# Gate and up projections as a seven-product block scheme, with the down projection as a stage of its own

## Chip, cores, metric
The kernel runs on one core of one Trainium2 chip. The metric is the device time of one execution in microseconds.

## What is computed
One decoder layer for 1024 tokens of width 1024, float32, with a feed-forward width of 2816. The change lies in the last part, the feed-forward network:

```
h = h + mixed @ w_out
u = h * rsqrt(mean(h*h) + eps) * norm2_gain
y = h + (silu(u @ w_gate) * (u @ w_up)) @ w_down
```

Before it come a first RMS norm, one input projection, a gated linear recurrence (4 heads) and a sliding-window attention (8 heads), whose outputs (`mixed`) meet in the output projection `w_out`.

## The kernel before
Activations lie transposed: features on the 128 partitions, in 8 tiles (`KT`), tokens along the free dimension, in two halves of 512. Every large product is done in three terms for precision: each operand is split into `hi` (rounded by an ACT copy to the fp32r type) and `lo` (the rest, by a DVE subtract), and `three()` (lines 759 to 763) issues hi\*hi, hi\*lo and lo\*hi into one PSUM bank of 128x512. PSUM has eight such banks.

The engines have separate programs. A list from `schedule()` sets one order of steps, and each engine walks through it and does its part of a step: `P` and `O` are input and output projection groups on PE, `LM`, `LX`, `LV`, `OC`, `OS`, `OM`, `ON`, `OX` the recurrence, `MS`/`ML` the hi and lo parts of a mixed tile, `FD`, `F` the load and the split of feed-forward weights. The output projection has 48 groups: 0 to 31 stand between the steps of the recurrence, 32 to 47 (one k-tile each, 3 matmuls) behind the last head. SP issues all DMAs in the order of the list.

From group 32 on, `N2` steps stand between the output groups: the first gate and up weights are multiplied with the k-tiles of `u` as they get ready. `u` here is h times the gain only. The norm's factor `nrs` for each token is found beside it (ACT squares, POOL sums, a matmul with ones, ACT Ln and Exp) and is multiplied onto the gate's result by DVE (line 1248) and, after Silu, by POOL once more for the up result (line 533).

The feed-forward network then is a loop of 11 passes (`ffn`), the first and last unrolled. A pass takes two of the 22 tiles of the feed-forward width: four weight tiles (gate, up, gate, up), each 8 k-tiles x 2 token halves x 3 terms = 48 matmuls; then the hidden product's hi and lo parts stay in SBUF, and the down projection adds both tiles into 16 banks' worth of output (96 matmuls), which DVE adds onto `h` (line 1270). 288 matmuls a pass. At the end eight tiles of y are stored.

Of the kernel before, what the change touches and what calls it, by code (L numbers as in the profile page):

```python
# [5 lines left out]
ALU = mybir.AluOpType  # L21
# [7 lines left out]
P = 128  # L29
D = 1024  # L30
# [27 lines left out]
def schedule():  # L58
# [79 lines left out]
    for h in range(NH):  # L138
# [58 lines left out]
def build(nc, xT, wv, wproj, wo_a, wo_b, wo_c, wg, wu, wd, gain1, gain2, lbl, ogain, qgain, kgain, sinks, yT):  # L197
    ctx = ExitStack()
    with ctx:
# [35 lines left out]
        h = at("h", 7, [P, KT, T])  # L235
# [48 lines left out]
        def on_tmp(hh):  # L284
# [4 lines left out]
        u2hi = at("u2hi", 39, [P, KT, T], F32R)  # L289
        u2lo = at("u2lo", 91, [P, KT, T], F32R)  # L290
        nsq = at("nsq", 79, [P, 2, T])
        nacc = at("nacc", 87, [P, T])
        nrs = at("nrs", 131, [P, T])
        hidhi = at("hidhi", 71, [P, 2, T], F32R)
        hidlo = at("hidlo", 79, [P, 2, T], F32R)
        gate = [at("gate01", 87, [P, 2, HALF]), at("gate23", 123, [P, 2, HALF])]
        hid = at("hid", 127, [P, 2, HALF])
        fraw = [at(f"fraw{p}", kb, [P, KT * P]) for p, kb in enumerate((187, 191, 155, 171, 179, 167))]
# [73 lines left out]
        def down_bank(first, g):  # L372

            return ((3, 4, 5, 6), (0, 1, 2, 7))[g // 4 % 2][g % 4] if first else g % 8

        def ffn_bank(first, p, half):

            return ((3, 4), (5, 6), (0, 1), (2, 7))[p][half] if first else 2 * p + half
# [4 lines left out]
        def _(sp):  # L383
# [7 lines left out]
            for step in order:  # L391
# [18 lines left out]
                if step[0] == "MS" and step[1] < 3 or step == ("W", N_PROJ + 1):  # L410

                    i = step[1] if step[1] < 3 else 3
                    sp.wait_ge(*((s_ufree, i + 1) if i < 3 else (s_pmm, 2 * N_PROJ)))
                    for k in (i,) if i < 3 else range(3, KT):
                        sp.dma_start(h[:, k, :], xv[k, :, :]).then_inc(s_x[k], 16)
                if step[0] == "FD":
                    p = step[1]

                    sp.wait_ge(*((s_on, 3), (s_kq, 8), (s_lmm, 2 * LEVELS * NH), (s_lmm, 2 * LEVELS * NH), (s_oc, 32), (s_on, 4))[p])
                    sp.dma_start(fraw[p][:, :], (wg[0], wu[0], wg[1], wu[1], wd[0], wd[1])[p]).then_inc(s_fraw[p], 16)  # L420
            with sp.Fori(0, FT // 2 - 1) as i:
                for p in range(6):
                    sp.wait_ge(s_flo, 6 * i + (p + 1))
                    w = (wg, wu, wg, wu, wd, wd)[p]
                    j = (0, 0, 1, 1, 0, 1)[p]
                    sp.dma_start(fraw[p][:, :], w[bass.ds(2 * i + (2 + j), 1), :, :].rearrange("a p n -> (a p) n"))\
                        .then_inc(s_fraw[p], 16)
# [7 lines left out]
        def _(pool):  # L435
            n0 = [0]
# [42 lines left out]
            for step in order:  # L479
# [28 lines left out]
                elif step[0] == "LV":  # L508
# [6 lines left out]
                    else:  # L515
# [4 lines left out]
                                            ALU.subtract).then_inc(s_lvs, 1)  # L520

            for m in range(1, KT):
                pool.wait_ge(s_nsq, m + 1)
                if m > 1:
                    pool.wait_ge(s_nacc, m - 1)
                nc.gpsimd.tensor_tensor(nacc[:, :], nacc[:, :], nsq[:, m % 2, :], ALU.add).then_inc(s_nacc, 1)
            pool.wait_ge(s_nrs, 1)
            with pool.Fori(0, FT // 2) as i:
                for j in range(2):
                    for half in range(2):  # L530
                        pool.wait_ge(s_silu, 4 * i + (2 * j + half + 1))
                        gv = gate[j][:, half, :]
                        nc.gpsimd.tensor_tensor(gv, gv, nrs[:, half * HALF:(half + 1) * HALF], ALU.mult)\  # L533
                            .then_inc(s_gr, 1)

        @block.scalar
        def _(act):
# [25 lines left out]
            def value_out(g):  # L563
                n, t = g // NC, g % NC
                act.wait_ge(s_vmm, g + 1)
                nc.scalar.activation(v[:, t, n * VW:(n + 1) * VW], ps[:, g % 8, 0:VW], ACT.Copy,
                                     scale=rtok[:, t:t + 1]).then_inc(s_vev, 1)

            for g in range(V_FIRST + 1):
                value_out(g)  # L570
            for step in order:
# [139 lines left out]
                elif kind == "NL":  # L711
                    m = step[1]
                    for x2, cols in first_in_halves(m):
                        act.wait_ge(s_oadd, 32 + 2 * m + x2)
                        nc.scalar.activation(u2hi[:, m, cols], h[:, m, cols], ACT.Copy, scale=g2[:, m:m + 1])\
                            .then_inc(s_u2hi, 1)
                    if m >= 3:
                        act.wait_ge(s_nacc, m - 2)
                    dst = nsq[:, m % 2, :] if m else nacc[:, :]
                    nc.scalar.activation(dst, h[:, m, :], ACT.Square).then_inc(s_nsq, 1)  # L720
                elif kind == "F":
                    p = step[1]
                    act.wait_ge(s_fraw[p], 16)

                    act.wait_ge(*((s_on, 3), (s_lmm, 2 * LEVELS * NH), (s_lmm, 2 * LEVELS * NH), (s_oc, 32), (s_on, 4), (s_omm, 48))[p])
                    nc.scalar.activation(fhi[p][:, :], fraw[p][:, :], ACT.Copy).then_inc(s_fhi, 1)

            act.wait_ge(s_nss, 2)
            nc.scalar.activation(nrs[:, 0:HALF], ps[:, 2, :], ACT.Ln, scale=1.0 / D, bias=eps).then_inc(s_nln, 1)
            nc.scalar.activation(nrs[:, HALF:T], ps[:, 7, :], ACT.Ln, scale=1.0 / D, bias=eps).then_inc(s_nln, 1)  # L730
            act.wait_ge(s_nln, 2)
            nc.scalar.activation(nrs[:, :], nrs[:, :], ACT.Exp, scale=-0.5).then_inc(s_nrs, 1)

            def ffn(i, last):

                for j in range(2):
                    for half in range(2):
                        act.wait_ge(s_gsc, 4 * i + (2 * j + half + 1))
                        nc.scalar.activation(gate[j][:, half, :], gate[j][:, half, :], ACT.Silu).then_inc(s_silu, 1)  # L739
                    for half in range(2):  # L740
                        act.wait_ge(s_hid, 4 * i + (2 * j + half + 1))
                        nc.scalar.activation(hidhi[:, j, half * HALF:(half + 1) * HALF], hid[:, half, :], ACT.Copy)\  # L742
                            .then_inc(s_hhi, 1)
                    for p in () if last else (2 * j, 2 * j + 1):
                        act.wait_ge(s_fraw[p], 16 * i + 32)
                        act.wait_ge(s_fmm, 8 * i + (2 * p + 2))
                        nc.scalar.activation(fhi[p][:, :], fraw[p][:, :], ACT.Copy).then_inc(s_fhi, 1)  # L747
                for p in () if last else (4, 5):
# [4 lines left out]
            with act.Fori(0, FT // 2 - 1) as i:  # L753
                ffn(i, False)
# [587 lines left out]
```

## Time and profile before

| | us |
|---|---|
| time, median of 3 runs | 1255.2 (1255.13 to 1256.24) |
| span of the profiled execution, first to last instruction | 1252.1 |
| PE busy | 1220.7 |
| DVE busy | 633.8 |
| ACT busy | 377.6 |
| POOL busy | 228.9 |

The profile is of one execution; its time is known only by its span, and the median of the runs is 3.1 us over that. PE is the matmul part of TensorE, DVE VectorE, ACT ScalarE, POOL GpSimd, SP the engine that issues DMAs. Busy times are sums of instructions; consecutive matmuls overlap, so a matmul's own duration (0.39 us) is longer than the distance to the next (0.23 us).

### The profile page before, as it was taken

The numbers are of one execution on the slowest core, as the hardware profiler recorded it, in microseconds if no ns is written. First come the engines' busy times: TensorE is split into PE (matmuls) and PEld (weight loads), VectorE is DVE, ScalarE is ACT, GpSimd is POOL, SyncE is SP. The second block draws the span as 40 slices with busy tenths as digits, with TensorE's granted clock in tenths as the row PEclk, the third lists the DMA queues.
The fourth block names the chain that finished last, engine by engine and source line by source line (L and its number), as shares of the span: only waits on it lengthen the run. The fifth ranks groups of instructions, "written<-read, shape, count | busy, mean of one in ns | idle before, by whom it ended". The sixth has DMA issues, their size and how long they took to land.

```text
span 1252.1 us, 14986 instructions
## 1 busy us (share of the span) xinstructions
PE 1220.7 (97%) x5840; PEld 1005.0 (80%) x5840; DVE 633.8 (51%) x832; ACT 377.6 (30%) x578; POOL 228.9 (18%) x155
## 2 busy tenths in 40 slices
PE   4999999999999999999999999999999999999998
PEld 4898766678888788778888888888888888888887
DVE  7305576577869795656343334343443425252514
ACT  6314454554545632452212121121212121121110
POOL 6301123342533330241100000000000000101010
PEclk9999999999999999999999999999999999999999
DMA  6101100000001302211101111011111211010003
GB/s 236 50 1 52 34 17 1 18 34 35 18 35 68 148 18 88 85 51 68 68 34 44 56 34 67 34 67 34 58 42 34 66 34 67 34 67 0 0 0 134
DMA packets 20056, 63.47 MB, mean 51 GB/s; under 512 B 3121, under 2 KB 5169, under 8 KB 20017
## 3 DMA queue, kind: packets, MB, share of 16 engines
q1 hardware_dynamic: 20016, 62.94, 14.3%
q8 instruction: 26, 0.43, 0.1%
q14 instruction: 14, 0.11, 0.0%
HBM read 58.74 MB, written 4.19 MB: 50 GB/s over the span
## 4 chain that ended last, share of the span: by engine, by line
PE 88%; DVE 5%; ACT 3%; issue 2%; POOL 1%; DMA 0%; SPq 0%; DVEq 0%; ACTq 0%
PE ps L761 27%; PE ps L763 26%; PE ps L762 26%; PE ps L927 4%; PE ps L888 1%; PE ps L902 1%; PE ps L903 1%; DVE ulo L1030 1%; DVE vlo L1024 1%; POOL D L519 1%; PE ps L953 1%; DVE B L1155 1%; POOL rec L507 0%; DVE M L1188 0%; DMA x<-xT 0%
## 5 line engine op out<-in xcount | busy, mean ns | idle before, releaser
L761 PE MATMUL ps<-u2hi,fhi 128*128 128x512 f32 x704 | 274.6, 390 | 0.9 <-DVE u2lo L1237 0.9
L763 PE MATMUL ps<-u2hi,flo 128*128 128x512 f32 x704 | 273.9, 389 | 0.0
L762 PE MATMUL ps<-u2lo,fhi 128*128 128x512 f32 x704 | 273.9, 389 | 0.0
L533 POOL TENSOR_TENSOR gate<-gate,nrs 128x512 f32<-128x512 f32 x44 | 56.7, 1291 | 612.3 <-ACT gate L739 612.3
L1270 DVE TENSOR_TENSOR h<-ps,h 128x512 f32<-128x512 f32 x176 | 116.9, 689 | 81.0 <-PE ps L763 81.0
L761 PEld LDWEIGHTS ps<-u2hi,fhi 128*128 128x128 f32 x704 | 132.2, 188 | 29.7 <-DVE u2lo L1237 1.4
L763 PEld LDWEIGHTS ps<-u2hi,flo 128*128 128x128 f32 x704 | 132.2, 188 | 27.5
L762 PEld LDWEIGHTS ps<-u2lo,fhi 128*128 128x128 f32 x704 | 132.2, 188 | 27.5 <-issue 0.2
L761 PE MATMUL ps<-hidhi,fhi 128*128 128x512 f32 x352 | 136.9, 389 | 0.0
L762 PE MATMUL ps<-hidlo,fhi 128*128 128x512 f32 x352 | 136.9, 389 | 0.0
L763 PE MATMUL ps<-hidhi,flo 128*128 128x512 f32 x352 | 136.9, 389 | 0.0
L1254 DVE TENSOR_TENSOR hid<-ps,gate 128x512 f32<-128x512 f32 x44 | 30.5, 692 | 196.8 <-PE ps L763 192.7
L761 PE MATMUL ps<-uhi,whi 128*128 128x512 f32 x272 | 112.3, 413 | 0.0
L763 PE MATMUL ps<-uhi,wlo 128*128 128x512 f32 x272 | 106.8, 393 | 0.0
L762 PE MATMUL ps<-ulo,whi 128*128 128x512 f32 x272 | 106.5, 392 | 0.0
L1248 DVE TENSOR_TENSOR gate<-ps,nrs 128x512 f32<-128x512 f32 x44 | 30.2, 691 | 131.1 <-PE ps L763 124.0
L742 ACT ACTIVATE hidhi<-hid 128x512 fp32r<-128x512 f32 x44 | 27.9, 633 | 199.1 <-DVE hid L1254 199.1
L1018 DVE TENSOR_TENSOR flo<-fraw,fhi 128x1024 fp32r<-128x1024 f32 x66 | 79.5, 1245 | 9.7 <-ACT fhi L747 5.1
L761 PEld LDWEIGHTS ps<-hidhi,fhi 128*128 128x128 f32 x352 | 66.1, 188 | 13.7
L763 PEld LDWEIGHTS ps<-hidhi,flo 128*128 128x128 f32 x352 | 66.1, 188 | 13.7
L762 PEld LDWEIGHTS ps<-hidlo,fhi 128*128 128x128 f32 x352 | 66.1, 188 | 13.7
L751 ACT ACTIVATE fhi<-fraw 128x1024 fp32r<-128x1024 f32 x20 | 20.1, 1052 | 184.2 <-PE ps L763 184.2
(192 smaller groups left out, 1876.8 us busy)
## 6 DMA issues: line engine op xcount, KB each, us to landing
fraw<-wu SPq DMA_DIRECT2D x22, 512.0 KB, 4.5
fraw<-wg SPq DMA_DIRECT2D x22, 512.0 KB, 3.2
fraw<-wd SPq DMA_DIRECT2D x22, 512.0 KB, 3.8
wraw<-wproj SPq DMA_DIRECT2D x17, 512.0 KB, 3.2
x<-xT SPq DMA_DIRECT2D x8, 512.0 KB, 6.9
h<-xT SPq DMA_DIRECT2D x8, 512.0 KB, 3.8
yT<-h SPq DMA_DIRECT2D x8, 512.0 KB, 2.6
vraw<-wv SPq DMA_DIRECT2D x16, 160.0 KB, 5.7
```

Of the source, the lines that this page charges most:

```text
L519: nc.gpsimd.tensor_tensor(DD[lv % 2][:, :].rearrange("p (b l) -> p b l", l=2 * L), b4, mid, ALU.subtract).then_inc(s_lvs, 1)
L533: nc.gpsimd.tensor_tensor(gv, gv, nrs[:, half * HALF:(half + 1) * HALF], ALU.mult)\
L742: nc.scalar.activation(hidhi[:, j, half * HALF:(half + 1) * HALF], hid[:, half, :], ACT.Copy)\
L751: nc.scalar.activation(fhi[p][:, :], fraw[p][:, :], ACT.Copy).then_inc(s_fhi, 1)
L761: nc.tensor.matmul(out, whi_, xhi_, start=first, stop=False)
L762: nc.tensor.matmul(out, whi_, xlo_, start=False, stop=False)
L763: return nc.tensor.matmul(out, wlo_, xhi_, start=False, stop=last)
L927: mm = nc.tensor.matmul(ps[:, 3 + c // 4, (c % 4) * P:(c % 4 + 1) * P], lhs[:, cs], rhs[:, cs], start=True, stop=True)
L1018: nc.vector.tensor_tensor(flo[p][:, :], fraw[p][:, :], fhi[p][:, :].bitcast(F32), ALU.subtract)\
L1248: nc.vector.tensor_tensor(gate[j][:, half, :], ps[:, ffn_bank(first, 2 * j, half), :], nrs[:, half * HALF:(half + 1) * HALF], ALU.mult).th ...
L1254: nc.vector.tensor_tensor(hid[:, half, :], ps[:, ffn_bank(first, 2 * j + 1, half), :], gate[j][:, half, :], ALU.mult).then_inc(s_hid, 1)
L1270: nc.vector.tensor_tensor(hv, ps[:, down_bank(first, g), :], hv, ALU.add)\
```

## The change
The 1024 features of `u` and of a weight tile are halved, and the tokens too: `u` becomes B11, B12 (features of the first half, tokens of each half) and B21, B22. A tile of gate weights gives A11, A12, one of up weights A21, A22. The four results (gate and up, for each token half) are formed from seven products of such blocks, each 4 k-tiles x 3 terms = 12 matmuls:

- the token side needs seven operands with hi and lo parts: B11, B21 as they are, B22, and four sums t1 = B12 - B11, t2 = B22 - t1, t3 = B22 - B12, t4 = B21 - t2. They are built once, after the norm, by DVE and POOL; so `u` is now normalised itself (`norm_tile`, and for B12 an ACT copy with the gain and a POOL multiply), in place over `h`, and `h` is first stored to HBM (`hD`) and read back later into `h2`;
- the weight side needs sums per tile: POOL forms four of 128x512 (`weight_sums`), ACT and DVE split them;
- a product that serves several results is made once and copied by ACT from one PSUM bank to the next (`seed_b`, `seed_c`); later products accumulate on the copy. `keep_p5` copies product 5 to SBUF, and DVE adds it to two results (`gate_2`, `up_2`).

The first two groups are interleaved while operands are being built; from the third on a group is (1,g) (4,g-1) (5,g) (6,g) (2,g) (3,g) (7,g). The hidden product goes to HBM (`hidD`), and the down projection comes after all gate/up groups, in 11 chunks of two tiles that are read back, split by ACT and DVE (`chunk_hi`, `chunk_lo`) and multiplied; DVE adds onto `h2`. All of it is unrolled. The `N2`, `NL`, `F`, `FD` steps go; `XU`/`XG` (loads), `XS` (POOL sums), `XH`/`XL`/`XA` (splits) take their place in the last head. Of the last 16 output groups the first token half comes first.

```diff
         if last:
-            steps[5] += [("FD", 1), ("FD", 0), ("MS", 6), ("ML", 6)]
+            steps[5] += [("XU", 0), ("XG", 0), ("MS", 6), ("ML", 6)]
             order += mix(take(n_p + 32 - taken[0]), steps)
-            order += [("FD", 2), ("FD", 3), ("F", 0)]
+            order += [("XS", 0)]
             steps = [[("OC", h, c)] for c in range(NC)] + ...
-            steps[2] += [("F", 1)]
-            steps[5] += [("F", 2)]
+            steps[2] += [("XH", 0)]
+            steps[3] += [("XL", 0)]
+            steps[8] += [("XA", 0), ("XG", 1), ("XU", 1)]
...
+    order += [("XS", 1), ("XH", 1)] + [("O", 32 + g, 0) for g in range(16)]
...
+        products = [(1, 0), (1, 1), (2, 0), (2, 1), (5, 0), (5, 1), (6, 0), (6, 1), (3, 0), (7, 0), (4, 0),
+                    (3, 1), (7, 1)]
+        for g in range(2, GROUPS):
+            products += [(1, g), (4, g - 1), (5, g), (6, g), (2, g), (3, g), (7, g)]
+        products += [(4, LAST)]
+            return ((3, 4, 5, 6), (0, 1, 2, 7))[g % 2]                # banks a, b, c, e
... POOL
+            def weight_sums(g):
...
+                nc.gpsimd.tensor_tensor(sw[:, 0:HALF], uw[:, 0:HALF], uw[:, HALF:D], ALU.add).then_inc(s_sum, 1)
+                nc.gpsimd.tensor_tensor(sw[:, HALF:D], sw[:, 0:HALF], gw[:, 0:HALF], ALU.subtract).then_inc(s_sum, 1)
+                nc.gpsimd.tensor_tensor(s34[:, 0:HALF], gw[:, 0:HALF], uw[:, 0:HALF], ALU.subtract).then_inc(s_sum, 1)
+                nc.gpsimd.tensor_tensor(s34[:, HALF:D], gw[:, HALF:D], sw[:, HALF:D], ALU.subtract).then_inc(s_sum, 1)
...
+            for k in range(4):
+                pool.wait_ge(s_unb, k + 1)
+                nc.gpsimd.tensor_tensor(h[:, 1, k, :], h[:, 1, k, :], nrs[:, 1, :], ALU.mult).then_inc(s_unp, 1)
... PE
+                bank = {1: a, 2: a, 3: c, 4: b, 5: e, 6: b, 7: b}[p]
+                elif p == 5:
+                    pe.wait_ge(s_12lo, g + 1)
+                elif p == 4:
+                    pe.wait_ge(s_22lo, g + 1)
+                    pe.wait_ge(s_c22, g + 1)
+            for p, g in products[4:]:
+                product_waits(p, g)
+                if (p, g) == (4, LAST):
+                    down(0, 0)
... output projection on PE
+                    if g == 43:
+                        norm_sum(0, (0, 6, 7), 5, 8)
+                    if g == 47:
+                        norm_sum(1, (0, 5, 6, 7), 9, 16)
... ACT, one group
+                s34_hi(g)
+                seed_b(g)
+                a22_hi(g)
+                keep_p5(g)
+                gate_hi(g + 1)
+                seed_c(g)
+                s12_hi(g + 1)
+                silu_1(g)
+                silu_2(g)
... DVE: the operands, then one group
+            norm_tile(0, 0)
+            for k in range(KT):
+                if k + 1 < KT:
+                    norm_tile(0, k + 1)
+                operand_lo(k // 4, k % 4, k % 4 + 1, h[:, 0, k, :], k + 1)
+                if k == 1:
+                    gate_lo(1)
+            for c in range(2): ... t1 ...
+            for k in range(2): norm_tile(1, 4 + k)
+            for c in range(2): operand_lo(4, ...)
+            for k in range(2, 4): norm_tile(1, 4 + k)
+            for c in range(2): ... t2 ...
+            s12_lo(1)
+            for c in range(2): operand_lo(5, ...)      # then 2, 6, 3 in the same way
...
+                s34_lo(g)
+                hid_1(g - 1)
+                a22_lo(g)
+                gate_lo(g + 1)
+                s12_lo(g + 1)
+                gate_2(g)
+                up_2(g)
```

## Rows read from the trace of the kernel before

**Rows 1.** The page: busy time, share of the span and instructions of each engine.
```profile
PE 1220.7 (97%) x5840; PEld 1005.0 (80%) x5840; DVE 633.8 (51%) x832; ACT 377.6 (30%) x578; POOL 228.9 (18%) x155
```
**Rows 2.** The page: the chain that ended last, by engine.
```profile
PE 88%; DVE 5%; ACT 3%; issue 2%; POOL 1%; DMA 0%; SPq 0%; DVEq 0%; ACTq 0%
```
**Rows 3.** PE's waits, 515 to 1249: total, times, longest.
```profile
PE ps L761 <- DVE u2lo L1237: 0.9, 2, 0.6
PE ps L761 <- DVE mlo L1232: 0.7, 1, 0.7
```
**Rows 4.** Timeline of PE: start, duration, operation, idle before.
```profile
515.64 0.47 PE L761 MATMUL ps<-mhi,whi 128*128 128x512 f32 x1 [0.69 <-DVE mlo L1232]
...
1248.00 0.39 PE L763 MATMUL ps<-hidhi,flo 128*128 128x512 f32 x1
```
**Rows 5.** Timeline of DVE: the last add group of two successive passes.
```profile
1181.19 2.65 DVE L1270 TENSOR_TENSOR h<-ps,h 128x512 f32<-128x512 f32 x4 [2.71 <-PE ps L763]
...
1246.38 2.73 DVE L1270 TENSOR_TENSOR h<-ps,h 128x512 f32<-128x512 f32 x4 [2.71 <-PE ps L763]
```
**Rows 6.** One pass: busy PE, PEld, DVE, ACT, POOL, clock, DMA share, GB/s.
```profile
1056.10:1121.30 65.20, 65.20 (x290) 53.99 (x289) 25.69 (x34) 12.15 (x15) 5.16 (x4) 1.00 0.14 48
```
**Rows 7.** Groups of ACT by shape: busy, mean ns, idle before.
```profile
L747 ACT ACTIVATE fhi<-fraw 128x1024 fp32r<-128x1024 f32 x40 | 39.8, 1043 | 0.0
L739 ACT ACTIVATE gate<-gate 128x512 f32<-128x512 f32 x44 | 27.7, 632 | 158.3 <-DVE gate L1248 158.3
L684 ACT ACTIVATE rec<-ps 128x512 f32<-128x512 f32 x8 | 4.7, 591 | 17.6 <-PE ps L947 17.6
```
**Rows 8.** Groups of DVE by shape.
```profile
L1048 DVE TENSOR_TENSOR wlo<-wraw,whi 128x1024 fp32r<-128x1024 f32 x22 | 28.2, 1285 | 10.8 <-ACT whi L579 10.8
L1248 DVE TENSOR_TENSOR gate<-ps,nrs 128x512 f32<-128x512 f32 x44 | 30.2, 691 | 131.1 <-PE ps L763 124.0 <-ACT nrs L732 7.1
```
**Rows 9.** Group of POOL by shape.
```profile
L533 POOL TENSOR_TENSOR gate<-gate,nrs 128x512 f32<-128x512 f32 x44 | 56.7, 1291 | 612.3 <-ACT gate L739 612.3
```
**Rows 10.** DMA issues: KB each, median us to landing.
```profile
fraw<-wu SPq DMA_DIRECT2D x22, 512.0 KB, 4.5
```
**Rows 11.** Timelines of POOL, then DVE, where both work.
```profile
440.09 1.89 POOL L519 TENSOR_TENSOR D<-B 128x1024 f32<-128x1024 f32 x1 [2.29 <-DVE rec L1179]
455.20 2.89 POOL L519 TENSOR_TENSOR D<-B 128x1024 f32<-128x1024 f32 x1 [1.23 <-DVE M L1188]
522.95 2.55 POOL L526 TENSOR_TENSOR nacc<-nacc,nsq 128x1024 f32<-128x1024 f32 x1 [64.86 <-ACT nsq L720]
...
440.53 2.00 DVE L1188 TENSOR_TENSOR M<-K,D 128x512 f32<-128x512 f32 x1
442.45 0.68 DVE L1188 TENSOR_TENSOR M<-Q,D 128x512 f32<-128x512 f32 x1
523.16 1.28 DVE L1089 TENSOR_TENSOR h<-ps,h 128x512 f32<-128x512 f32 x2
```
**Rows 12.** Group of DVE in 10 to 34 us.
```profile
L1030 DVE SCALAR_TENSOR_TENSOR ulo<-x,small,uhi 128x1024 fp32r<-128x1024 f32 x6 | 14.1, 2356 | 0.6 <-ACT uhi L545 0.6
```
**Rows 13.** The chain in order of time: start, duration.
```profile
555.74 1.72 PE ps L989 x4
```
**Rows 14.** Two stretches; columns as in rows 6.
```profile
20.00:24.00 4.00, 1.32 (x7) 1.35 (x8) 4.00 (x2) 4.00 (x6) 3.86 (x2) 0.93 0.54 200
24.00:28.00 4.00, 2.35 (x9) 1.95 (x8) 4.00 (x2) 0.39 (x1) 3.71 (x3) 0.64 0.14 41
```
**Rows 15.** The last head: timelines of DVE and PE.
```profile
487.92 0.69 DVE L1089 TENSOR_TENSOR h<-ps,h 128x512 f32<-128x512 f32 x1 [1.80 <-PE ps L763]
489.50 0.35 DVE L1207 SCALAR_TENSOR_TENSOR S<-S,small,ps 128x128 f32<-128x128 f32 x1
...
489.53 0.39 PE L947 MATMUL ps<-X,S 128*128 128x128 f32 x2
```
**Rows 16.** One stretch; the last column is GB/s.
```profile
8.00:20.00 12.00, 9.22 (x45) 8.76 (x45) 11.38 (x7) 12.00 (x17) 9.11 (x4) 1.00 1.02 385
```

More of the change, by code:

```diff
@@ L286, in on_tmp @@
             return (X0, X0, rawf, M[0])[hh]
[L289 to L298, printed above, removed]
@@ L370, in out_bank, with out_tile, banks, up_buffer @@
             return (2 * N_PROJ + g) % 3 if g < 32 else (0, 1, 2, 7)[g % 4]
[L372 to L378, printed above, removed]
+        def out_tile(g):
+            return (g % 16 // 2, g % 2) if g < 32 else (g % 8, (g - 32) // 8)
+        GROUPS = FT
+        LAST = GROUPS - 1
+        CHUNKS = FT // 2
+        products = [(1, 0), (1, 1), (2, 0), (2, 1), (5, 0), (5, 1), (6, 0), (6, 1), (3, 0), (7, 0), (4, 0),
[3 more added lines that the diff above has]
+        products += [(4, LAST)]
+        done = {pg: i + 1 for i, pg in enumerate(products)}
+        def banks(g):
+            return ((3, 4, 5, 6), (0, 1, 2, 7))[g % 2]
+        def up_buffer(g):
+            return (1, g // 2) if g >= 2 and g % 2 == 0 else (0, (g + 1) // 2 + 1)
         block = ctx.enter_context(nc.Block())
@@ L421, in _ @@
[L421 to L427, printed above, removed]
+                    for k in (2 * i, 2 * i + 1):
+                        sp.dma_start(h[:, :, k, :], xv[k, :, :].rearrange("p (x t) -> p x t", x=2)).then_inc(s_x[k], 16)
@@ L728, in _ @@
[L728 to L734, printed above, removed]
-                for j in range(2):
[L737 to L748, printed above, removed]
-                    act.wait_ge(s_fraw[p], 16 * i + 32)
-                    act.wait_ge(s_dmm, 16 * i + 16)
-                    nc.scalar.activation(fhi[p][:, :], fraw[p][:, :], ACT.Copy).then_inc(s_fhi, 1)
@@ new lines, in operand_hi, with b12_gain, seed_b @@
+            def operand_hi(i, c0, c1, src):
+                nc.scalar.activation(ohi[i][:, c0:c1, :], src, ACT.Copy).then_inc(s_ohi, 1)
+            def b12_gain(k):
+                if k == 0:
+                    act.wait_ge(s_hst[1], 16 * KT)
+                nc.scalar.activation(h[:, 1, k, :], h[:, 1, k, :], ACT.Copy, scale=g2[:, k:k + 1]).then_inc(s_unb, 1)
+            def seed_b(g):
+                a, b, c, e = banks(g)
+                act.wait_ge(s_prod, done[1, g])
+                if g >= 2:
+                    act.wait_ge(s_hid1, g - 1)
+                nc.scalar.activation(ps[:, b, :], ps[:, a, :], ACT.Copy).then_inc(s_seedb, 1)
@@ L757, in _, with three @@
+            for i in range(1, CHUNKS):
+                for j in range(2):
+                    chunk_hi(i, j)
         @block.tensor
         def _(pe):
-            def three(out, whi_, wlo_, xhi_, xlo_, first, last):
-                nc.tensor.matmul(out, whi_, xhi_, start=first, stop=False)
-                nc.tensor.matmul(out, whi_, xlo_, start=False, stop=False)
-                return nc.tensor.matmul(out, wlo_, xhi_, start=False, stop=last)
+            def three(out, whi_, wlo_, xhi_, xlo_, first, last, seeded=False):
+                nc.tensor.matmul(out, whi_, xhi_, start=first, stop=False, skip_group_check=seeded)
+                nc.tensor.matmul(out, whi_, xlo_, start=False, stop=False, skip_group_check=seeded)
+                return nc.tensor.matmul(out, wlo_, xhi_, start=False, stop=last, skip_group_check=seeded)
@@ L770, in value_part, with down, norm_sum @@
                              k == 0, k == KT - 1)
+            def down(i, q):
+                for j in range(2):
+                    if q == 0:
+                        pe.wait_ge(s_hlo, 2 * i + j + 1)
+                        pe.wait_ge(s_dlo, 2 * i + j + 1)
+                    for b in range(4):
+                        n = 4 * i + q
+                        m, half = 2 * q + b // 2, b % 2
+                        if j == 0 and n < 2 and b == 0:
+                            g = LAST - 1 + n
+                            pe.wait_ge(s_sg1, g + 1)
+                            pe.wait_ge(s_hid1, g + 1)
+                            pe.wait_ge(s_c12, g + 1)
+                            pe.wait_ge(s_p5s, g + 1)
+                        if j == 0 and n >= 2:
+                            pe.wait_ge(s_dadd, 4 * (n - 2) + b + 1)
+                        w = slice(m * P, (m + 1) * P)
+                        t = slice(half * HALF, (half + 1) * HALF)
+                        mm = three(ps[:, banks(q)[b], :], dhi[i % 3][:, j, w], dlo[i % 3][:, j, w], hhi[i % 3][:, j, t],
+                                   hlo[i % 3][:, j, t], j == 0, j == 1)
+                        if j:
+                            mm.then_inc(s_dmm, 1)
+            def norm_sum(x, tiles_, added, squares):
+                pe.wait_ge(s_nacc, added)
+                pe.wait_ge(s_nsq, squares)
+                for m in tiles_:
+                    mm = nc.tensor.matmul(ps[:, 4 + x, :], ones[:, :], nsq[:, x, m, :], start=m == 0, stop=m == 7)
+                mm.then_inc(s_nss, 1)
             pe.wait_ge(s_pool0, 2)
@@ L1009, in _, with product_part @@
-            ffn(0, True)
-            with pe.Fori(1, FT // 2) as i:
-                ffn(i, False)
+            def product_part(p, g, k):
+                a, b, c, e = banks(g)
+                bank = {1: a, 2: a, 3: c, 4: b, 5: e, 6: b, 7: b}[p]
+                first = slice(k * P, (k + 1) * P)
+                second = slice(HALF + k * P, HALF + (k + 1) * P)
+                if p in (1, 2):
+                    w = first if p == 1 else second
+                    w_hi, w_lo = ghi[g % 2][:, w], glo[g % 2][:, w]
+                elif p in (5, 6):
+                    w = first if p == 5 else second
+                    w_hi, w_lo = s12hi[g % 2][:, w], s12lo[g % 2][:, w]
+                elif p in (3, 7):
+                    w = second if p == 3 else first
+                    w_hi, w_lo = s34hi[:, w], s34lo[:, w]
+                else:
+                    w_hi, w_lo = ahi[:, first], alo[:, first]
+                fresh = p in (1, 5)
+                mm = three(ps[:, bank, :], w_hi, w_lo, ohi[p - 1][:, k, :], olo[p - 1][:, k, :], fresh and k == 0,
+                           k == 3, seeded=not fresh)
+                if k == 3:
+                    mm.then_inc(s_prod, 1)
@@ L1013, in _, with gate_lo @@
+            for n in range(1, 4 * CHUNKS):
+                down(n // 4, n % 4)
         @block.vector
         def _(dve):
-            def ffn_weights_lo(p, n):
-                dve.wait_ge(s_fhi, n)
-                nc.vector.tensor_tensor(flo[p][:, :], fraw[p][:, :], fhi[p][:, :].bitcast(F32), ALU.subtract)\
-                    .then_inc(s_flo, 1)
+            def gate_lo(g):
+                dve.wait_ge(s_ghi, g + 1)
+                dve.wait_ge(s_sum, 4 * g + 4)
+                nc.vector.tensor_tensor(glo[g % 2][:, :], graw[g % 2][:, :], ghi[g % 2][:, :].bitcast(F32), ALU.subtract)\
+                    .then_inc(s_glo, 1)
@@ new lines, in operand_lo, with hid_1 @@
+            def operand_lo(i, c0, c1, src, n):
+                dve.wait_ge(s_ohi, n)
+                nc.vector.tensor_tensor(olo[i][:, c0:c1, :], src, ohi[i][:, c0:c1, :].bitcast(F32), ALU.subtract)\
+                    .then_inc(s_olo, 1)
+            def hid_1(g):
+                dve.wait_ge(s_prod, done[4, g])
+                dve.wait_ge(s_sg1, g + 1)
+                if g >= 2:
+                    dve.wait_ge(s_hidout[g % 2], 16 * (g // 2))
+                if g == 0:
+                    dve.wait_ge(s_t4, 2)
+                nc.vector.tensor_tensor(hidst[g % 2][:, 0, :], ps[:, banks(g)[1], :], sg1[:, :], ALU.mult)\
+                    .then_inc(s_hid1, 1)
@@ new lines, in gate_2, with up_2 @@
+            def gate_2(g):
+                dve.wait_ge(s_prod, done[3, g])
+                dve.wait_ge(s_p5s, g + 1)
+                if g:
+                    dve.wait_ge(s_hid2, g)
+                nc.vector.tensor_tensor(sg2[:, :], ps[:, banks(g)[2], :], p5s[:, :], ALU.add).then_inc(s_c12, 1)
+            def up_2(g):
+                dve.wait_ge(s_prod, done[7, g])
+                if g:
+                    dve.wait_ge(s_hid2, g)
+                nc.vector.tensor_tensor(upg[:, :], ps[:, banks(g)[1], :], p5s[:, :], ALU.add).then_inc(s_c22, 1)
@@ new lines, in _ @@
+            up_2(0)
+            s34_lo(1)
+            hid_1(0)
+            a22_lo(1)
+            gate_lo(2)
+            gate_2(1)
+            s12_lo(2)
+            up_2(1)
+            for g in range(2, GROUPS):
+                s34_lo(g)
+                hid_1(g - 1)
+                a22_lo(g)
+                if g < LAST:
+                    gate_lo(g + 1)
+                    s12_lo(g + 1)
+                else:
+                    for j in range(2):
+                        chunk_lo(0, j)
+                gate_2(g)
+                up_2(g)
@@ new lines, in down_add @@
+            def down_add(i, q):
+                for b in range(4):
+                    m, x = 2 * q + b // 2, b % 2
+                    dve.wait_ge(s_dmm, 16 * i + 4 * q + b + 1)
+                    if i == 0 and b == 0:
+                        dve.wait_ge(s_h2[q], 64)
+                    if i:
+                        dve.wait_ge(s_dadd, 16 * (i - 1) + 4 * q + b + 1)
+                    nc.vector.tensor_tensor(h2[:, x, m, :], ps[:, banks(q)[b], :], h2[:, x, m, :], ALU.add)\
+                        .then_inc(s_dadd, 1)
@@ L1281 @@
+            hid_1(LAST)
+            for i in range(CHUNKS):
+                for q in range(4):
+                    down_add(i, q)
+                    if i + 1 < CHUNKS and q in (1, 2):
+                        chunk_lo(i + 1, q - 1)
 def kernel(x, norm1_gain, w_in, hgrn_lb_logits, hgrn_out_gain, q_norm_gain, k_norm_gain, attn_sinks, w_out,
```

498 lines of the change are left out of this document (350 added, 148 removed).

## The prediction, made before the result was known
> **What bounds the kernel now.** I read the page's busy shares first, then the chain of waits, then PE's waits in the feed-forward stage, then single rows. PE is busy 1220.7 of 1252.1 us and no other engine passes 51% [rows 1]; the chain is 88% PE [rows 2]. From the first matmul of the last third of the output projection (515.64) PE waits 0.9 + 0.7 us in all until the end [rows 3], and the last matmul starts at 1248.00 [rows 4]. So this stretch is 732.8 us of PE work: 48 matmuls of the output projection, 2112 of gate/up, 1056 of down. One loop pass of 288 matmuls takes 65.2 us: the last add group of a pass starts at 1181.19, that of the next at 1246.38 [rows 5], at full clock [rows 6]: 0.2264 us per matmul. In one pass DVE is busy 25.7, ACT 12.2, POOL 5.2 us, so all have room.
>
> The span is 1252.1 us and the runs' median 1255.2, so 3.1 us lie around the span. The sum is made on the span, and 3.1 are added. A difference under 0.2% (2.5 us) I call no change.
>
> **What the change removes.** Gate and up are each a 1024-deep product; together a 2x2 block matrix times a 2x2 block matrix. Eight block products of 12 matmuls (4 k-tiles, 3 precision terms) become seven. 22 tiles x 12 = 264 matmuls fewer, x 0.2264 = **59.8 us**. This is the ceiling. Removed as well, at nothing since all of it lies beside PE: the gate scaling (POOL 56.7 us, DVE 30.2) [rows 8, 9], the hi/lo split of the product in place, the loop.
>
> **Added in the steady part.** PE spends 84 x 0.2264 = 19.0 us on a group of 7 products (2.7 us each). I lay each engine's queue against it.
> - ACT: three 128x1024 copies (1.04), one 128x512 copy, three PSUM-sourced copies, two Silu (0.60 to 0.63 each) [rows 7]: 6.9 us. A copy from PSUM to PSUM isn't in the trace. Bounds: 0.59, the eviction to SBUF of this size, and 1.04, the copy twice as large; I take 0.65. Even 1.04 fits: a seed is needed 5.4 us (bank b) or 2.7 us (bank c) after its source is done, and what can stand before it is one 1.04 copy.
> - DVE: three 128x1024 subtracts (1.22), one 128x512, and three PSUM-fed (0.69) [rows 8]: 6.4 us.
> - POOL: five 128x512 operations at 1.29 [rows 9]: 6.5 us.
> - SP: three DMAs of 512 KB per 19 us, landing in 4.5 us [rows 10]; the next gate tile is issued when product 2 ends, 5.4 us before the group's end, and is first read behind that.
> The tightest release is up_2: it must read bank b after product 7 and before product 4 goes into that bank, with one product between: 2.7 us against about 0.9 (0.69 and the hop of 0.2). No group should wait. Cost 0; 141 products from the third group on take 141 x 12 x 0.2264 = 383.1 us.
>
> **The transition, where the price is.** Before, gate/up starts on un-normalised columns (the scale is applied after), so PE fills the norm with gate/up matmuls. Now operands are sums of normalised tiles: seven hi/lo pairs must exist, and the first waits for the norm. I lay it out, from O32's start as 0.
> A rule is needed first. While POOL runs an SBUF operation (440.09 to 441.98), a DVE operation with two SBUF inputs that takes 0.68 otherwise starts at 440.53 and ends at 442.53: it stood until POOL was through. The reverse: POOL's subtract of 455.20, in the row under it, takes 2.89 instead of 1.89. A DVE add fed from PSUM keeps 0.69 beside POOL (523.16, two in 1.28) [rows 11]. In 10 to 34 us, both engines' queues full, DVE's 128x1024 operations average 2.36 us against 1.28 [rows 12]. So I queue two-input DVE and POOL operations one after the other, alternating. The Trainium skill, SBUF — State Buffer, section "Who interferes with whom", says it as a rule: with two SBUF inputs on DVE against a POOL read, the second to issue waits out the first. By that rule the transition ends at 79; if both ran freely, at 65, as below. The trace agrees with it (440.53 ends after 441.98).
> 1. PE runs O32 to O43 (12 x 0.68) to 8.1. POOL finishes the sums of the second weight tile at 3.9 and then five norm adds of 1.3: 10.4. PE waits 2.4. Three ones-matmuls at 0.86 (a pair took 1.72 on the chain [rows 13]) to 13.1; O44 to O47 to 15.8.
> 2. ACT is held by the first Ln/Exp (0.69 + 0.69) until 14.6, its squares then let POOL end at 17.9; PE waits 2.2; four ones-matmuls to 21.4.
> 3. Products 1 and 2 of both groups (48 matmuls, 10.9 us) eat a k-tile per 1.36 us. Each needs a DVE normalise and a subtract (1.3 together), an ACT copy, and beside them ACT does the second Ln/Exp and POOL four multiplies (1.27) that block DVE. Ends 37.1 instead of 32.3: 4.8 waited.
> 4. Product 5 waits for t1 (two 1.2 subtracts), two normalises and its own subtract: first half 39.8, second 43.5 behind POOL's t3 (2.55): 2.7 + 2.3 waited.
> 5. Product 5 of the second group waits for s12_lo(1), which stands on DVE behind two normalises, two t2 and, by the lock, one t3 and one t4 half (2.55 each): 53.3, while PE was through at 44.9: **8.4** waited.
> 6. Products 6, 3, 7: 1.1 waited, then DVE keeps ahead. Product 4 of group 0 stands straight behind product 7 on the same bank: 0.9.
> PE is through the 13 products at 77. Idle this long costs clock as well: the stretch 24 to 28, after PE's starved 20 to 24, shows a granted clock of 0.64, the 1.2 GHz level for most of it [rows 14]; at half the clock a matmul's 0.2264 doubles, some 0.2 more each. I add 2.0 for ten such. **79** for 204 matmuls (46.2) and seven ones-matmuls (6.0): 26.8 of loss. Bounds for it: 12.6 (no lock: the same list gives waits of 2.0, 2.4, 1.0, 2.8, 3.4 and 1.0, PE through at 65) and 40 (the 1.2 GHz level on half of the 156 product matmuls, 78 x 0.2 = 15.6 instead of 2.0).
>
> **Head.** In the last head DVE now does three weight subtracts in a lump (3 x 1.18) at 486.05, behind the state update of 485.79. The add of 487.92 comes at 489.6 and the update of 489.50 at 491.2, for which PE's chunk matmul at 489.53 waits [rows 15]: 2.0 us. POOL's second weight sum shares the port with the last mix subtract: 0.2. Bounds 0 and 3.7 (the whole lump); I take **2.2**.
>
> **Seam to down.** PE waits for up_2 of the last group before it starts down: DVE has the four chunk subtracts ahead of it, which wait for ACT's four copies: 21.5 against 19.0 in that group: 2.5. Then the second quarter of down waits for hid_1 of the last group: 0.8. Chunk 1 is read from HBM only when the last product is through, 17 us ahead of its use; 2 MB take 5.5 us at the 385 GB/s of 8 to 20 us and twice that at half the rate [rows 16], and ACT and DVE 2.3 more: hidden. **3.3**, bounds 0.8 and 10 (chunk 1 late). Down's 1056 matmuls: 239.1. Per chunk DVE works 16 x 0.69 + 4 x 1.22 = 16 of 21.7 us, ACT 4.2: no wait. The tail (last add, store of 2.6) is as it was.
>
> **Sum.** 2.2 + 79 + 383.1 + 3.3 + 239.1 = 706.7 against 732.8: 26.1 less. Span 1226.0, time **1229.1**.
>
> **Rivals.**
> - A, the engines overlap better in the transition (lock ties fall PE's way, or s12_lo(1) gets through before POOL's halves): PE through at 65 instead of 79, time 1215. For it: which of two waiting engines goes first isn't shown where both wait. Against: rows 12. Chance 0.27 (1208 to 1221).
> - B, the transition is worse: the idle PE keeps the 1.2 GHz level over the whole of the first two groups, or chunk 1 comes late. With the bounds 40 and 10: 13.2 + 6.7 on top, 1249.0. Chance 0.13 (1238 to 1252).
> - C, slower: a wait in each group. Its place is product 4, released by up_2 on DVE. If DVE is held by the lock (gate_lo or s12_lo behind POOL's four sums) so that up_2 comes 3.0 us later than I have it, each of 20 groups waits 1.3 and the gain is gone; at 2 us each the time is 1229 + 40 = 1269. Against it: DVE and POOL together are 12.9 of 19.0 us per group even in a row, and what stands right before up_2 is fed from PSUM. Chance 0.07 for over 1257.7.
> - D, nothing is left within 2.5 us: 0.03.
> The forecast keeps 0.50 (1221 to 1238). Range: A and B are taken in until 0.2 is out: 1211 to 1244. Faster 0.90, same 0.03, slower 0.07.
>
> **What would show it.** PE rows of gate/up count 1848 at the same spacing; PE's waits list the DVE operand subtracts and s12_lo with one wait near 8 us; granted clock drops once or twice right behind 515, nowhere later; a group of 84 matmuls takes 19.0 us with DVE, ACT, POOL each near 6.5; PE's last O matmul at about 2 us later than now. If groups take over 19.3, rival C is at work; if PE's waits behind 515 sum to under 15, rival A.

## The result and the profile after

The changed kernel takes 1238.15 us (median of 4 runs, 1235.59 to 1239.72) against 1255.49 (4 runs) for the kernel before: ratio 0.985, 95% interval 0.9826 to 0.9873. It is 17.3 us faster. The forecast was 1229.1 in a range of 1211 to 1244. The profiled execution took 1235.6, its span 1233.6: 18.5 under the span before, where the sum had 26.1.

Page of the changed kernel: busy time and share, and below it the chain by engine, against [rows 1, 2].

```profile
PE 1176.6 (95%) x5586; PEld 963.7 (78%) x5586; DVE 721.8 (59%) x857; ACT 445.3 (36%) x679; POOL 354.2 (29%) x231
...
PE 84%; POOL 5%; DVE 4%; ACT 4%; issue 3%; DMA 1%; SPq 0%; POOLq 0%; DVEq 0%; ACTq 0%
```

PE is busy 44 us less, not 60. Most of the difference stands behind 520 us: where the granted clock is down, matmuls follow each other at 0.43 us (521.25, 521.67, 522.10) instead of 0.23, and the first matmul behind a wait is longer too. The span shrinks by 18.5, so PE now idles more. Where, its waits from 440 us on say (total, times, longest), against [rows 3]:

```profile
PE ps L978 <- DVE s12lo L1280: 9.3, 1, 9.3
PE ps L978 <- DVE olo L1520: 5.7, 4, 2.5
PE ps L978 <- issue: 3.9, 3, 2.3
PE ps L978 <- DVE mlo L1504: 3.9, 1, 3.9
PE ps L978 <- DVE glo L1274: 2.6, 1, 2.6
PE ps L1017 <- POOL nsq L628: 2.0, 1, 2.0
PE ps L1017 <- POOL nsq L623: 0.7, 1, 0.7
```

Every one of them stands between 516 and 600 us or at the seam to the down projection; in between, and in the down projection, there is none. The places on PE's timeline (start, duration, operation, idle before), against [rows 4]: start of the last output groups, product 5 of the second group, product 1 of the third, and the two halves of the seam; last, the final matmul.

```profile
520.10 0.47 PE L978 MATMUL ps<-mhi,whi 128*128 128x512 f32 x1 [3.86 <-DVE mlo L1504]
572.04 0.79 PE L978 MATMUL ps<-ohi,s12hi 128*128 128x512 f32 x1 [9.25 <-DVE s12lo L1280]
599.43 0.80 PE L978 MATMUL ps<-ohi,ghi 128*128 128x512 f32 x1 [2.63 <-DVE glo L1274]
984.36 0.47 PE L978 MATMUL ps<-hhi,dhi 128*128 128x512 f32 x1 [2.27 <-issue]
995.23 0.47 PE L978 MATMUL ps<-hhi,dhi 128*128 128x512 f32 x1 [0.83 <-issue]
...
1229.05 0.39 PE L980 MATMUL ps<-hhi,dlo 128*128 128x512 f32 x1
```

Stretches of the changed kernel (PE, PEld, DVE, ACT, POOL busy, granted clock, DMA share, GB/s), against [rows 6, 14]. The third column from the end is the clock: it is below 1 behind or within each of the four longer waits (3.86, 9.25, 2.63, 2.27), and 1 in the steady part, where PE is busy all the time as before.

```profile
515.00:530.00 15.00, 11.14 (x42) 8.53 (x40) 12.88 (x17) 9.08 (x13) 11.56 (x9) 0.89 0.38 146
560.00:570.00 10.00, 2.78 (x12) 1.96 (x11) 10.00 (x6) 2.34 (x3) 8.65 (x3) 0.76 0.10 34
570.00:580.00 10.00, 7.96 (x28) 6.46 (x29) 10.00 (x7) 4.14 (x6) 4.22 (x2) 0.72 0.18 71
600.00:610.00 10.00, 10.00 (x40) 8.15 (x39) 4.47 (x5) 3.31 (x6) 7.62 (x5) 0.86 0.04 4
700.00:800.00 100.00, 100.00 (x443) 82.81 (x442) 41.58 (x37) 33.74 (x47) 43.48 (x29) 1.00 0.27 79
980.00:1000.00 20.00, 16.89 (x67) 13.18 (x66) 8.38 (x12) 2.94 (x4) 1.29 (x1) 0.91 0.64 229
```

DVE (first) and POOL in the transition, against [rows 11]:

```profile
560.73 3.54 DVE L1515 SCALAR_TENSOR_TENSOR h<-h,small,nrs 128x512 f32<-128x512 f32 x2
564.19 4.50 DVE L1575 TENSOR_TENSOR t<-h,t 128x1024 f32<-128x1024 f32 x2
568.61 3.37 DVE L1280 TENSOR_TENSOR s12lo<-s12raw,s12hi 128x1024 fp32r<-128x1024 f32 x1
571.91 4.53 DVE L1520 TENSOR_TENSOR olo<-t,ohi 128x1024 fp32r<-128x1024 f32 x2
...
558.68 4.38 POOL L637 TENSOR_TENSOR t<-h 128x1024 f32<-128x1024 f32 x1 [6.34 <-DVE h L1515]
564.41 3.19 POOL L637 TENSOR_TENSOR t<-h 128x1024 f32<-128x1024 f32 x1 [1.35 <-DVE h L1515]
567.57 6.66 POOL L643 TENSOR_TENSOR t<-h,t 128x1024 f32<-128x1024 f32 x2
```

Both engines look full, but much of their busy time is standing: a DVE subtract of 1.2 us takes 3.37, and a POOL subtract of 128x1024 takes 3.19 to 4.38, where a POOL operation of this size took 2.55 in [rows 11]. Each stands while the other has the turn. DVE is busy 10.00 of 10 us in 560 to 570 and in 570 to 580, so it is not waiting for POOL's results there; it is held inside its own instructions.

### The profile page after: what moved, and what is told of

It reads as the page before. It is cut to its first block, busy times and chain, and to the rows that moved or that the text cites. A ratio compares the mean times of both kernels' runs of the same rounds, so it can differ in the third digit from the quotient of the medians.

```text
span 1233.6 us, 14293 instructions
## 1 busy us (share of the span) xinstructions
PE 1176.6 (95%) x5586; PEld 963.7 (78%) x5586; DVE 721.8 (59%) x857; ACT 445.3 (36%) x679; POOL 354.2 (29%) x231
## 4 chain that ended last, share of the span: by engine, by line
PE 84%; POOL 5%; DVE 4%; ACT 4%; issue 3%; DMA 1%; SPq 0%; POOLq 0%; DVEq 0%; ACTq 0%
PE ps L978 25%; PE ps L979 24%; PE ps L980 24%; PE ps L1178 4%; POOL sq L548 2%; PE ps L1139 1%; PE ps L1153 1%; PE ps L1154 1%; DVE h L1515 1%; POOL D L614 1%; DVE B L1427 1%; PE ps L1017 1%; DMA wraw<-wo_c 0%; DVE olo L1520 0%; PE ps L1204 0%
## 5 line engine op out<-in xcount | busy, mean ns | idle before, releaser
L978 PE MATMUL ps<-hhi,dhi 128*128 128x512 f32 x352 | 137.8, 392 | 3.1 <-issue 3.1
L979 PE MATMUL ps<-hlo,dhi 128*128 128x512 f32 x352 | 137.6, 391 | 0.0
L980 PE MATMUL ps<-hhi,dlo 128*128 128x512 f32 x352 | 137.5, 391 | 0.0
L978 PE MATMUL ps<-ohi,s12hi 128*128 128x512 f32 x176 | 69.4, 395 | 11.7 <-DVE s12lo L1280 9.3
L978 PEld LDWEIGHTS ps<-hhi,dhi 128*128 128x128 f32 x352 | 66.4, 189 | 17.7 <-issue 3.9
L978 PE MATMUL ps<-ohi,ghi 128*128 128x512 f32 x176 | 70.2, 399 | 5.8 <-DVE olo L1520 3.2
L979 PE MATMUL ps<-olo,s12hi 128*128 128x512 f32 x176 | 69.1, 393 | 0.0
L979 PE MATMUL ps<-olo,ghi 128*128 128x512 f32 x176 | 69.1, 393 | 0.0
L980 PE MATMUL ps<-ohi,glo 128*128 128x512 f32 x176 | 69.0, 392 | 0.0
L980 PE MATMUL ps<-ohi,s12lo 128*128 128x512 f32 x176 | 68.9, 392 | 0.0
L978 PE MATMUL ps<-ohi,s34hi 128*128 128x512 f32 x176 | 68.5, 389 | 0.0
```

Source lines behind the costliest of these rows:

```text
L978: nc.tensor.matmul(out, whi_, xhi_, start=first, stop=False, skip_group_check=seeded)
L979: nc.tensor.matmul(out, whi_, xlo_, start=False, stop=False, skip_group_check=seeded)
L980: return nc.tensor.matmul(out, wlo_, xhi_, start=False, stop=last, skip_group_check=seeded)
```

## Experiments

All times are medians; a1 is the base. Single executions of one kernel spread by 3 to 9 us here, so a difference under 2 us between medians is read from the trace, not from the clock on the wall.

**a1: the changed kernel again.** 

> The changed kernel once more, unchanged, as the base for the others: 1238 us within 2.

 Measured 1235.8 (5 runs; ratio to before 0.9842, 0.9824 to 0.986). From the first matmul of the last output groups to the first of the third product group: 520.27 to 602.20, 81.9 us. The same stretch took 79.3 (520.10 to 599.43) in the first profiled execution of the same kernel. 1.7 of the difference is eight records of the ones-matmuls, 5.40 us instead of 3.70, at a lower clock, and 1.1 lies behind the 7.7 us wait (28.5 instead of 27.4 us to the third group). So a change in this stretch that is under 3 us is within what one kernel shows.

**a2: one engine instead of two.**

```
-  (POOL) 4 x tensor_tensor(h[:,1,k,:], ..., nrs, mult); 2 x t3 = B22 - B12; 2 x t4 = B21 - t2
+  (DVE)  the same eight operations: the multiplies ahead of t1, t3 behind operand_lo(5), t4 behind operand_lo(2)
```

> In the transition the four multiplies of B12 by the norm factor, t3 and t4 move from POOL to DVE; nothing else changes. Theory queue (a DVE operation with two SBUF inputs and a POOL operation run one after the other): DVE gains 4 x 0.6 + 4 x 1.2 = 7.2 us of work and loses the blocking by POOL's 4 x 1.3 + 4 x 2.55 = 15.4 us; the 13 products end 4 to 8 us earlier, DVE's subtract of 128x1024 takes 1.22 all through the stretch, time 1231 to 1234. Theory free (the two engines overlap, POOL took work off DVE): the products end up to 7 us later, 1245.

 Measured 1226.56 (1225.05 to 1228.83; ratio to before 0.9773, 0.9756 to 0.9791): 9.2 us faster than a1, a little more than the theory of one queue had, and opposite to the rival. The stretch of 81.9 us is 72.0 (518.81 to 590.78); a1 is the fair comparison, as its ones-matmuls took 5.40 us too. Timeline of DVE in a2; the first row is t1, the others are the operations of the second to fourth DVE row above:

```profile
554.29 2.36 DVE L1552 TENSOR_TENSOR t<-h 128x1024 f32<-128x1024 f32 x2
561.48 2.35 DVE L1563 TENSOR_TENSOR t<-h,t 128x1024 f32<-128x1024 f32 x2
563.75 1.22 DVE L1264 TENSOR_TENSOR s12lo<-s12raw,s12hi 128x1024 fp32r<-128x1024 f32 x1
564.88 2.36 DVE L1504 TENSOR_TENSOR olo<-t,ohi 128x1024 fp32r<-128x1024 f32 x2
```

DVE does more work in less time: 1.2 us each, back to back. Giving work to an idle engine had made the busy one slower.

**a3: order of loads on SP.**

```
-  steps[8] += [("XA", 0), ("XG", 1), ("XU", 1)]
+  steps[8] += [("XA", 0)]
-  order += [("XS", 1), ("XH", 1)] + ...
+  order += [("XG", 1), ("XU", 1), ("XS", 1), ("XH", 1)] + ...
```

> The loads of the second gate and up weight tile are issued by SP behind the last output weights instead of ahead of them. Theory order: the copy that split the last output weights waited for that DMA at 511.7 us and held the last head's norm on ACT; PE's wait of 3.9 us for the last mixed tile falls to 0.7 as before, O32 starts 3.2 us earlier, 1235. Rival lump (the three weight subtracts on DVE delay the chain): the wait stays, 1238.

 In the changed kernel SP issues the last output weights at 506.07 (done at 507.47), behind the second up tile, which had to wait for its buffer until 505.70. ACT, which splits the output weights on its way to the last head's norm, waits for them. The first two rows are SP's, the third ACT's in the changed kernel, the last two ACT's and PE's in a3:

```profile
505.70 0.33 SPq L445 DMA_DIRECT2D uraw<-wu  x1
506.07 1.40 SPq L426 DMA_DIRECT2D wraw<-wo_c  x1
511.70 1.06 ACT L724 ACTIVATE whi<-wraw 128x1024 fp32r<-128x1024 f32 x1 [7.94 <-DMA wraw<-wo_c]
...
507.64 1.06 ACT L724 ACTIVATE whi<-wraw 128x1024 fp32r<-128x1024 f32 x1 [2.66 <-PE ps L980]
518.36 0.47 PE L978 MATMUL ps<-mhi,whi 128*128 128x512 f32 x1 [0.89 <-DVE mlo L1504]
```

PE's wait falls from 3.86 to 0.89, so theory "order" holds for the wait: measured from the add on DVE four groups earlier (499.51 in the changed kernel, 500.11 in a1, 500.74 in a3), the last groups start 17.6 us later instead of 20.6 (20.2 in a1). The rival falls: the lump of three subtracts, still there, delays nothing. From the start of the last groups to the ones-matmuls it is 10.5 us in a1 and in a3, though PE's wait there is 0.5 in a1 and 2.1 in a3 (clock 0.89 and 0.98 in 515 to 530): POOL's sums set this stretch. The way to the third group is 81.7 (81.9 in a1), and the profiled execution keeps the gain, a span of 1232.6 for 1234.9. But the median of the times is 1235.83 (1233.19 to 1241.67), none won against a1; with a spread of 8.5 us over six runs it neither shows the gain nor rules it out.

**a4: the seam.**

```
-  product_waits(p, g);  if (p, g) == (4, LAST): down(0, 0)
+  if (p, g) == (4, LAST): down(0, 0);  product_waits(p, g)
```

> On PE the first quarter of the down projection goes ahead of the waits of the last product 4 instead of behind them. Theory: the wait of 2.3 us at 984 us goes and with it the fall of the granted clock right behind it, which costs 1.7: 1234.5 to 1236. Rival: the wait moves to the chunk's second tile or to product 4 and nothing is won, 1238.

 Measured 1234.46 (1231.86 to 1235.03). PE's only wait left there is the 0.83 at 994.50; from the third group's start to that point it takes 391.7 us against 394.3 in a1, 2.6 less, of which 2.4 is the wait itself. The clock did not fall at the seam in a1, so this pair says nothing of that part of the theory. By the medians alone, 1.3, the gain is not settled.

**b1: the eighth product back.**

```
+  for again in range(2 if p == 5 and g >= 2 else 1): ... product 5, restarted in its bank
```

> From the third group on product 5 is issued twice (the second time afresh, so the result stays): 8 block products of 12 matmuls again in 20 of 22 groups, all else as changed. Theory PE-bound groups: 20 x 12 x 0.2264 = 54.3 us more, 1290 us, which is 35 over the kernel before: the price of all that the scheme adds. Rival (other engines or a queue bound the groups too): less than 40 us more.

 Measured 1292.15 (ratio to before 1.0281, 1.0258 to 1.0304): 56.4 over a1, for 54.3 expected, and the rival's "less than 40" is out. With an eighth product PE stays just as busy:

```profile
650.00:850.00 200.00, 200.00 (x884) 165.68 (x883) 73.90 (x65) 61.02 (x83) 72.51 (x47) 1.00 0.24 72
```

So a group costs what PE's matmuls cost. The expectation took 35 us for the price of all that the scheme adds; that is too low, since b1 still leaves out the eighth product in the first two groups, 24 matmuls or 5.4 us. b1 is 36.6 us over the kernel before, so the machinery (normalised operands, HBM round trip, seam) costs about 42 us. The changed kernel says the same: 59.8 less the 17.3 that it won is 42.5.

**b2: the one long wait, moved.**

```
   if k == 1: gate_lo(1)
+             s12_lo(1)        # instead of behind t2
```

> Of the changed kernel only DVE's subtract for the second group's s12 weights (s12_lo(1)) is moved up, from behind t2 to behind gate_lo(1). Theory queue (the transition ends when DVE and POOL have worked off their common queue): PE's wait of 7.6 to 9.3 us for s12_lo goes but comes back as waits for the operand subtracts behind it; the 13 products end within 2 us of now, 1235 to 1237. Rival (that one wait is the loss): 8 us won, 1228.

 Measured 1234.77 (1231.71 to 1237.51). The wait for s12_lo is gone, and product 5 of the second group starts at once. The next product now waits for its operand instead, at nearly the same distance from the start of the last groups (53.5 us; the wait for s12_lo ended at 51.9 in the changed kernel and 53.4 in a1):

```profile
578.00 0.76 PE L978 MATMUL ps<-ohi,s12hi 128*128 128x512 f32 x1 [6.61 <-DVE olo L1520]
```

DVE ends its last operand subtract 63.5 us after the start of the last groups, 63.3 in the changed kernel: moving one operation within the queue does not shorten it, as the queue theory says. The stretch is 78.4 us, 0.9 and 3.5 under the two traces of the changed kernel, and the median 1.0 under a1: neither is clear of the spread, and both are far from the rival's 8.

**b3: the wait filled.**

```
+  if (p, g) == (5, 1):
+      36 x matmul(ps[bank e of group 1], ghi[0], ohi[0], start=True, stop=True)
```

> Of the changed kernel only PE's long wait before product 5 of the second group is filled with 36 matmuls of no use (8.1 us) into the bank that this product clears. Theory clock: PE's waits let the granted clock fall to 1.2 GHz for 13.6 us in 560 to 590, which costs products 5 and 6 some 2 us; filled, it stays at 2.4 GHz there and the 13 products end 2 us earlier, 1234. Rival (PE waits there for DVE anyway): no change, 1236, with the fall gone.

 Measured 1235.71 (1234.47 to 1238.47): no change by the median. 560 to 590 in the changed kernel and in b3:

```profile
560.00:590.00 30.00, 19.91 (x79) 15.73 (x79) 25.94 (x17) 11.82 (x13) 12.87 (x4) 0.83 0.09 35
```

```profile
560.00:590.00 30.00, 26.38 (x113) 20.94 (x114) 26.84 (x18) 11.26 (x13) 14.34 (x4) 1.00 0.10 36
```

The clock stays up there. What came of it is to be read from product 5 of the second group to product 1 of the third, in a1 and then in b3:

```profile
573.67 0.79 PE L978 MATMUL ps<-ohi,s12hi 128*128 128x512 f32 x1 [7.71 <-DVE s12lo L1280]
602.20 0.50 PE L978 MATMUL ps<-ohi,ghi 128*128 128x512 f32 x1 [2.59 <-DVE glo L1274]
...
573.53 0.50 PE L978 MATMUL ps<-ohi,s12hi 128*128 128x512 f32 x1 [1.19 <-DVE s12lo L1283]
600.01 0.50 PE L978 MATMUL ps<-ohi,ghi 128*128 128x512 f32 x1 [2.61 <-DVE glo L1277]
```

28.5 us in a1, 26.5 in b3, 27.4 in the first trace of the changed kernel: 0.9 to 2.1 came back behind the wait, near the 2 of theory "clock". Of that, 0.9 is lost again ahead of the ones-matmuls, a place that the edit does not touch (11.5 us from the start of the last groups, 10.5 in a1), so the whole stretch is 80.9 for 81.9. The rival's reason, that PE would have waited for DVE anyway, is not borne out behind the wait: b3 has one wait of 0.42 for an operand there. It does hold ahead of the wait: in a1 the clock was down in the last seven matmuls before it (562.77 to 565.33), and the wait was 7.7 instead of 9.25. A gain of 1 to 2 us is too small for these medians, so the run does not decide between the two theories by time.

**b4: together.** The edits of a2, a3, a4, and POOL's weight sums of the third group ahead of its first hidden product:

```
-  if 1 <= g < LAST: weight_sums(g + 1)
+  if g == 0: weight_sums(2)
+  elif 2 <= g < LAST: weight_sums(g + 1)
```

> Four edits together: the multiplies, t3 and t4 on DVE (as a2), the weight loads behind the output weights (as a3), down's first quarter ahead of product 4's waits (as a4), and POOL's weight sums of the third group ahead of its first hidden product. By the first three alone 9.2 + 1.5 + 1.5: 1223.6; the fourth should take away PE's wait of 2.5 us for glo(2) and the fall of the clock behind it (1.7): 1220. If the waits only shift, 1224.

 Measured 1218.13 (1213.91 to 1221.84; ratio to before 0.9701, 0.9677 to 0.9724), 17.7 under a1 and 2 under the lower of the two forecasts. PE's waits from 440 us on:

```profile
PE ps L964 <- DVE olo L1506: 5.2, 2, 4.9
PE ps L1003 <- POOL nsq L623: 2.1, 1, 2.1
PE ps L1003 <- POOL nsq L628: 2.0, 1, 2.0
PE ps L964 <- issue: 1.8, 2, 0.9
PE ps L964 <- DVE mlo L1490: 0.9, 1, 0.9
PE ps L964 <- DVE s12lo L1266: 0.3, 1, 0.3
```

The wait for glo(2) and the first of the two at the seam are gone (the second, 0.83, stays at 977.86), and no fall of the clock stands at either place (1.00 in 580 to 620 and in 975 to 1005). From product 1 of the third group to the last matmul b4 takes 623.8 us and a2 628.0. The four edits were not tried in other combinations, so what the fourth alone is worth is not measured. b4 beats the kernel before by 37.5 us, about twice what the change did.

## Why the prediction came out

**Ceiling and steady part: right.** 264 matmuls fewer at an unchanged distance; the eighth product put back costs 56.4 us (20 of 22 groups) where the price of a matmul gives 54.3. No group waits between the start of the third and the seam. DVE is busy 7.9 us of a 19.0 us group (41.58 of 100) and POOL 8.3, for 6.4 and 6.5 forecast: the surplus is turns waited for, hidden by PE (from 620 to 980 DVE's `s34lo` takes 2.04 us for 1.22 alone, POOL's first sum 2.27 for 1.29). A copy from PSUM to PSUM takes 0.58, I had 0.65. Rival C did not come.

**Transition: the mechanism right, the closeness of the number in part luck.** 79 was forecast, 79.3 came (520.10 to 599.43; 81.9, 81.7 and 81.8 in a1, a3 and a4). The forecast's longest wait, 8.4 for s12_lo(1) by two-input DVE and POOL operations taking turns, is 9.25. a2 shows the reason and a size: eight operations on POOL cost 10.0 us there (81.9 less 72.0). But the terms offset each other. The waits sum to 21.1 where 24.8 was forecast: for the norm sums 2.7 (4.6 forecast), in products 1 and 2 3.2 (4.8), at product 5 2.5 (5.0), for s12_lo 9.25 (8.4), at products 6 to 4 0.8 (2.0), and for glo(2), the lo part of the third group's gate weights, 2.6, which the forecast put at nothing. That last one is POOL's order: it sums the third group's weights behind its first hidden product, and DVE's subtract for glo(2) waits for these sums. The rows are that product, the last of the sums, and DVE's subtract:

```profile
591.21 1.30 POOL L652 TENSOR_TENSOR hidst<-sg,up 128x512 f32<-128x512 f32 x1 [16.99 <-ACT sg L910]
596.79 1.26 POOL L529 TENSOR_TENSOR s34raw<-graw,s12raw 128x512 f32<-128x512 f32 x1
598.15 1.22 DVE L1274 TENSOR_TENSOR glo<-graw,ghi 128x1024 fp32r<-128x1024 f32 x1 [5.10 <-POOL s34raw L529]
```

The clock was to cost 2.0 in one place; the matmuls at 0.43 us cost 3.3 in two (520.87 to 524.51, 572.04 to 575.58). The rest, about 3 us, is lost in starting again behind waits and ones-matmuls, where the first matmul stands 0.3 to 0.6 us ahead of the next instead of 0.23; no term was there for it.

**Seam: the waits right and for the reason given, the clock missing.** 2.5 and 0.8 forecast, 2.27 and 0.83 found. DVE does the four chunk subtracts (978.26 to 983.06) ahead of up_2, which ends at 984.26, and PE starts at 984.36. Chunk 1 was in time. But the clock fell behind the first wait (0.91 in 980 to 1000), and 36 matmuls took 10.0 us beside the second wait instead of 8.15: 1.9 more. 1.6 of it is the fall: up to the second quarter's first matmul it took 10.87 us, where a1, with the clock at 1.00, took 9.26 (987.27 to 996.53).

**Head: size near, reason wrong.** The step that failed is the lump of subtracts: 2.0 was to come from the state update behind it. That was a misreading of [rows 15] already: the chunk matmul at 489.53 starts before the update of 489.50, 0.35 us long, is over, so it does not wait for it. In the changed kernel the same matmul stands at 490.82 and the update at 492.20, and the next chunk's matmul, 492.97 before, stands at 494.26: both 1.3 later, so the lump cost PE nothing. What cost 3.2 was the order on SP: the output weights' DMA behind the wait of the second up tile, which the prediction never looked at (a3). The start of the last groups was 4.5 late, for 2.2 forecast; the other 1.3 stood there before the lump. It begins behind a wait of 2.24 us at 434.86, where the clock fell, in code that the change did not touch.

**Sum.** 7.6 us of gain less than forecast: 1.3 that fall, 1.0 head, 0.3 transition, 2.3 the products behind it (140 x 12 took 382.7, not 380.4; 1.7 of it is matmuls at 0.43 us behind the wait for glo(2), clock 0.86 in 600 to 610), 1.7 the seam (1.9 of slower matmuls, 0.2 of shorter wait), 0.4 down, 0.5 the tail. Some 4.6 us of it is one term, mis-sized: the clock behind waits of 2.2 to 2.6 us at 435, 599 and 984, for which the forecast had nothing; it had said that the clock drops nowhere later than right behind 515. Why the same wait is followed by a fall in one execution and not in another stays open.

## What to carry to other kernels

A scheme with fewer matmuls pays in full only where PE stays the bound; look at the start and the seams, where its operands must be built before PE can begin. There, count two-input DVE work and POOL work as one queue: what is moved from POOL onto a full DVE can shorten the whole, as a2 did by 9.2 us. And when a DMA step is put into a fixed order, ask what each later DMA of that queue was for.

## What was not expected of the hardware

- The granted clock fell behind waits of only 2.1 to 2.6 us on PE, but not each time. Of the ten traces here, eight have a fall behind the wait of 2.25 us at 433 to 441 (not the kernel before and b3). Eight have the wait of 2.5 to 2.6 us for glo(2), seven with a fall (not b2). Seven have the wait of 2.1 to 2.4 us at the seam, three with a fall (the first trace, b1, b2). The two that were priced cost 1.6 (seam) and 1.7 us (third group), with PE as the bound. What came at the lower clock ahead of a long wait was taken off the wait (7.7 instead of 9.25 in a1).
- Eight POOL operations, 15.4 us by themselves, run beside DVE, cost the path more than the 7.2 us that DVE needs for them: 9.2 us were won by giving them back.
